# One decoder layer on one core: the output projection for prompt tile 0 first, for the rest behind two heads' queries

## The chip, the cores and the metric

One Trainium2 chip, of which the kernel uses one core. The metric is device time in microseconds, from the first to the last instruction and what lies around them, as the median of several executions. Engines are called as the profile calls them: PE (TensorE), DVE (VectorE), ACT (ScalarE), POOL (GpSimd), SP (SyncE, here only a queue of transfers).

## The reference, cut to what matters

A prompt of 256 tokens and 8 samples of one token each go through a layer of width 2048, all in f32. Three branches (a gated convolution, differential attention, attention to a memory) are gated and merged; the output projection adds them to x. Then comes PEER: queries and key scores select, for each token and each of 8 heads, 16 of 16384 experts; each expert is a row of `peer_u` and a row of `peer_v`, 8 KB each.

```python
x = x + merged @ w_o
h = rms_norm(x, norm2_w)
q = (h @ w_peer_q).reshape(n, 8, 2, 128)          # 2 x 128 per head
s1, s2 = q[:, :, 0] . sub_keys[0], q[:, :, 1] . sub_keys[1]
idx, top_s = 16 best sums of the 16 best of s1 and of s2, for each head
a = peer_u[idx] . h                                # a gathered row per token and pick
out = sum over heads and picks of softmax(top_s) * gelu(a) * peer_v[idx]
x = x + out
```

## The kernel before, in words

The 264 tokens stand as tile 0 and tile 1 of the prompt (128 each) and a tile of 8 samples. The program of each engine is written by hand; engines wait for each other on counting semaphores. The change lies behind the branches, where these parts follow each other:

- **Output projection** (PE L997 to L1003, with `chunk` L689 and `turner` L744). `w_o` comes in 8 blocks of 256 columns (2 MB) through `wring`, a ring of two slots; SP fetches block n when the second chunk of block n-2 is done (L361 to L369). A chunk is 128 output columns: 16 matmuls of 264 tokens, transposed, into a bank of `ps`. ACT copies it to `zst` (L1318), DVE adds it to the kept columns of x in `hT` (L1904) and ACT scales `hT` with the norm weight (L1321): these are the queries' operand. PE turns `zst` back to rows (three transposes), which DVE adds to `x_rows` and squares for the second norm (L1915 to L1921).
- **Queries and scores** (PE L1016 to L1038, ACT `stage_part` and `keep_scores` L1327 to L1350). `w_peer_q` has 8 blocks too, one for each head, two chunks j each (j = 2h and 2h+1). `PQ_PARTS` (L237) is their order: head 0 for tile 0, head 0 for the rest, then all heads for all tokens. Blocks 0 and 3 are loaded early into `bregion` and `oreg`, 4 and 7 into `late_h2`, the others through the ring. Each chunk is copied to `zst` by ACT, multiplied with the keys (L1013), and the scores are copied to `scores`. ACT does this in program order, and only then goes on to `winners(0)`, an exponential (L1362), and `activations(0)`, a Gelu (L1355).
- **Searches** (DVE, `search_halves`, `form_sums`, `search_sums`, `name_next`, L1966 to L2016) find the 16 experts of a head for a tile, and run between the dots, in four steps. Heads of tile 0 are g = 0 to 7, of tile 1 g = 8 to 15.
- **Gathers** (POOL L556 to L612). For each g and pick j an indirect DMA brings 128 rows of `peer_u` (1 MB) into one of four slots (`u_slots`), if the slot's earlier dot is done (`u_used`). Rows of `peer_v` go to eight slots (`e_slots`), which are parts of the weight ring, `oreg` and `hT`, so the first of them wait for query blocks (L578). Rows of v run behind those of u: `v_before` (L276), with `V_LEAD` 34. Both are issued by one program, in one order. The samples have 8 gathers of each kind of their own.
- **Dots and additions**. DVE forms the dot of each gathered u tile with `h2_rows` (L2049); `weigh(g)` (L2033) makes a head's weights from the exponential and the Gelu. The first, `weigh(0)`, stands behind the first dot of g = 2 (L2078). ACT makes a diagonal matrix of each pick's weights (L1385), PE multiplies the v rows with it and adds up in `ps` (L1057).

The second norm of tile 1 and the samples is finished at g = 5 (`late_norms`, L1933), from norm weights that SP loads over query block 7 (L386).

## Time and profile before

| | |
|---|---|
| median of 3 runs | 2703.18 us (2702.1 to 2703.5) |
| the profiled execution | 2701.93 us, span 2700.2 us |
| busy | PE 2428.8 us (90%), DVE 1474.5 (55%), ACT 349.4 (13%), POOL 806.9 (30%) |
| granted TensorE clock, mean | 0.973 |
| moved by DMA | 919.23 MB, 340 GB/s; the gather queue (q0) 725.64 MB |
| chain that ended last | PE 52%, DMA 36%, DVE 8% |

How it is read: the busy share of an engine is a mean over stages with different limits, and PE's share in particular is modelled: in the stage of the gathers its matmuls are stretched over waits. A window's row has, for one stretch of time, the busy time of each engine with its number of instructions, the granted TensorE clock (1.00 is 2.4 GHz, 0.50 is 1.2 GHz), the share of the 16 DMA engines and the rate. A row of the timeline has start, duration, engine, line, operation, written and read tile, count, and in brackets the idle time ahead of it and what ended it. A matmul in f32 stands as two records. DMA queue q0 carries the gathers, q1 the transfers that SP issues.

### The profile page before, as it was taken

The numbers are of one execution on the slowest core, as the hardware profiler recorded it, in microseconds if no ns is written. First come the engines' busy times: TensorE is split into PE (matmuls) and PEld (weight loads), VectorE is DVE, ScalarE is ACT, GpSimd is POOL, SyncE is SP. The second block draws the span as 40 slices with busy tenths as digits, with TensorE's granted clock in tenths as the row PEclk, the third lists the DMA queues.
The fourth block names the chain that finished last, engine by engine and source line by source line (L and its number), as shares of the span: only waits on it lengthen the run. The fifth ranks groups of instructions, "written<-read, shape, count | busy, mean of one in ns | idle before, by whom it ended". The sixth has DMA issues, their size and how long they took to land.

```text
span 2700.2 us, 27156 instructions
## 1 busy us (share of the span) xinstructions
PE 2428.8 (90%) x8845; PEld 1510.1 (56%) x8845; DVE 1474.5 (55%) x2290; ACT 349.4 (13%) x773; POOL 806.9 (30%) x889
## 2 busy tenths in 40 slices
PE   9999999999999999999997777777999597777778
PEld 7888886478666688888884322333433142223333
DVE  3599996842322231012487778874555555554543
ACT  2111000022222200001112110111101011111100
POOL 1122220101222200000146444544434454344442
PEclk9999999999999999999999999998989799999989
DMA  6699995865899945456599999999999999999998
GB/s 229 219 400 385 384 383 199 310 218 179 312 357 361 362 152 190 140 183 212 195 392 371 421 421 422 421 421 421 421 421 421 391 422 422 421 421 421 421 421 350
DMA packets 269444, 919.23 MB, mean 340 GB/s; under 512 B 16155, under 2 KB 122739, under 8 KB 200309
## 3 DMA queue, kind: packets, MB, share of 16 engines
q0 software_dynamic: 122448, 725.64, 66.2%
q1 hardware_dynamic: 133156, 164.93, 18.2%
q10 hardware_dynamic: 13728, 27.26, 2.7%
q8 instruction: 59, 0.97, 0.1%
q14 instruction: 53, 0.43, 0.0%
HBM read 909.08 MB, written 8.72 MB: 340 GB/s over the span
## 4 chain that ended last, share of the span: by engine, by line
PE 52%; DMA 36%; DVE 8%; issue 3%; POOL 1%; ACT 0%; DVEq 0%; POOLq 0%; ACTq 0%; SPq 0%
DMA sb_bregion<-in_peer_u_dram,sb_ring 27%; PE ps L699 13%; PE ps L807 13%; PE ps L819 6%; DVE sb_bregion L2049 4%; PE ps L689 4%; PE ps L794 4%; PE ps L1057 4%; DMA sb_mkv<-in_peer_u_dram,sb_ring 2%; PE ps L908 2%; DMA sb_S<-in_peer_u_dram,sb_ring 2%; DMA sb_wring<-in_w_in_dram 2%; DMA sb_bregion<-in_peer_v_dram,sb_ring 1%; PE ps L1031 1%; DVE sb_mkv L2049 1%
## 5 line engine op out<-in xcount | busy, mean ns | idle before, releaser
L1057 PE MATMUL ps<-sb_wring,sb_ring 128*128 128x512 f32 x992 | 456.0, 609 | 84.5 <-DMA sb_wring<-in_peer_v_dram,sb_ring 84.4
L2049 DVE CUSTOM_DVE_ANT_0 sb_bregion<-sb_bregion,sb_rows 128x2048 f32<-128x2048 f32 x128 | 293.4, 2292 | 218.5 <-DMA sb_bregion<-in_peer_u_dram,sb_ring 215.2
L699 PE MATMUL ps<-sb_hT,sb_wring 128*128 128x264 f32 x1792 | 408.2, 388 | 0.9 <-DMA sb_wring<-in_w_in_dram 0.8
L1057 PEld LDWEIGHTS ps<-sb_wring,sb_ring 128*128 128x128 f32 x992 | 185.5, 193 | 353.3 <-issue 255.3
L699 PEld LDWEIGHTS ps<-sb_hT,sb_wring 128*128 128x128 f32 x1792 | 338.6, 191 | 60.2 <-DMA sb_wring<-in_w_in_dram 2.4
L807 PE MATMUL ps<-sb_hT,sb_wring 128*128 128x264 f32 x1536 | 365.6, 389 | 1.1 <-DVEq L1418 1.1
L807 PEld LDWEIGHTS ps<-sb_hT,sb_wring 128*128 128x128 f32 x1536 | 286.4, 190 | 64.1 <-issue 16.4
L1057 PE MATMUL ps<-sb_oreg,sb_ring 128*128 128x512 f32 x496 | 236.0, 626 | 71.1 <-DMA sb_oreg<-in_peer_v_dram,sb_ring 42.8
L1057 PE MATMUL ps<-sb_hT,sb_ring 128*128 128x512 f32 x496 | 229.7, 610 | 52.0 <-DMA sb_hT<-in_peer_v_dram,sb_ring 46.7
L558 POOL DMA_INDIRECT sb_bregion<-in_peer_u_dram,sb_ring x132 | 152.1, 1152 | 328.4 <-DVEq L1418 289.7
L1385 ACT ACTIVATE sb_ring<-sb_ident,sb_ring 128x128 f32<-128x128 f32 x248 | 99.6, 401 | 912.9 <-PE ps L1057 746.5
L1057 PEld LDWEIGHTS ps<-sb_oreg,sb_ring 128*128 128x128 f32 x496 | 96.3, 200 | 209.9 <-issue 137.3
L2049 DVE CUSTOM_DVE_ANT_0 sb_S<-sb_S,sb_rows 128x2048 f32<-128x2048 f32 x64 | 146.7, 2292 | 109.7 <-DMA sb_S<-in_peer_u_dram,sb_ring 108.9
L2049 DVE CUSTOM_DVE_ANT_0 sb_mkv<-sb_mkv,sb_rows 128x2048 f32<-128x2048 f32 x64 | 147.1, 2298 | 104.3 <-DMA sb_mkv<-in_peer_u_dram,sb_ring 102.5
L1057 PEld LDWEIGHTS ps<-sb_hT,sb_ring 128*128 128x128 f32 x496 | 92.6, 193 | 187.4 <-issue 154.3
L558 POOL DMA_INDIRECT sb_wring<-in_peer_v_dram,sb_ring x128 | 156.8, 1225 | 51.5 <-issue 40.0
L1546 DVE TENSOR_REDUCE sb_S<-sb_oreg 128x1024 f32 x128 | 149.5, 1208 | 0.0
L819 PE MATMUL ps<-sb_oreg,sb_bregion 128*128 128x264 f32 x512 | 122.1, 388 | 0.0
L689 PE MATMUL ps<-sb_conv,sb_wring 128*128 128x264 f32 x512 | 116.4, 386 | 0.0
L558 POOL DMA_INDIRECT sb_S<-in_peer_u_dram,sb_ring x66 | 73.2, 1109 | 126.5 <-DVEq L1418 104.9
L819 PEld LDWEIGHTS ps<-sb_oreg,sb_bregion 128*128 128x128 f32 x512 | 96.4, 190 | 25.4 <-issue 9.4
L592 POOL COPY sb_ring<-sb_ring 128x16 int32<-128x16 int32 x16 | 18.2, 1140 | 308.5 <-DVEq L1418 308.4
(368 smaller groups left out, 2519.2 us busy)
## 6 DMA issues: line engine op xcount, KB each, us to landing
sb_wring<-in_w_in_dram SPq DMA_DIRECT2D x26, 2048.0 KB, 11.8
sb_ring<-in_cache_k_dram POOLq DMA_DIRECT2D x64, 512.0 KB, 8.5
sb_mkv<-in_cache_k_dram POOLq DMA_DIRECT2D x64, 512.0 KB, 8.5
sb_wring<-in_w_in_dram SPq DMA_DIRECT2D x26, 1024.0 KB, 12.8
sb_wring<-in_w_in_dram ACTq DMA_DIRECT2D x26, 1024.0 KB, 14.0
sb_mkv<-in_cache_v_dram POOLq DMA_DIRECT2D x48, 512.0 KB, 7.1
sb_rows<-in_cache_v_dram POOLq DMA_DIRECT2D x47, 512.0 KB, 7.6
sb_wring<-in_w_mem_kv_dram SPq DMA_DIRECT2D x8, 2048.0 KB, 8.6
```

Source lines behind the costliest of these rows:

```text
L558: nc.gpsimd.indirect_dma_start(dst, None, table, bass.IndirectOffsetOnAxis(ap=idx, axis=0)).then_inc(landed, 16)
L689: last = mm(ps[:, (2 * r + c) % 4, 0:NT], wring[:, r, k, c * P:(c + 1) * P], rhs[:, k, :], start=(k == 0), stop=(k == KC - 1))
L699: last = mm(ps[:, c, 0:NT], whalf[:, h, k % BC, c * P:(c + 1) * P], rhs[:, k, :], start=(k == 0), stop=(k == KC - 1))
L794: last = mm(ps[:, 2 * g + t, :], memT[:, k, t * P:(t + 1) * P], whalf[:, h, k % BC, :], start=(k == 0), stop=(k == KC - 1))
L807: last = mm(ps[:, c, 0:NT], wring[:, r, k, c * P:(c + 1) * P], hT[:, k, :], start=(k == 0), stop=(k == KC - 1))
L819: last = mm(ps[:, bank, 0:NT], bwring[:, r, k, c * P:(c + 1) * P], operand[:, k, :], start=(k == 0), stop=(k == BC - 1))
L908: last = mm(ps[g * QUAD:g * QUAD + w.shape[1], 6 + q, :], w, v_slots[page_slot(p)][:, q * 512:(q + 1) * 512], start=first, stop=final)
L1031: last = mm(ps[:, i % 4, lo:hi], pq_block(b, k)[:, c * P:(c + 1) * P], hT[:, k, lo:hi], start=(k == 0), stop=(k == KC - 1))
L1057: last = mm(ps[:, 4 * t + q, :], diag[:, k % 4, :], e_slots[v % ER][:, q * 512:(q + 1) * 512], start=False, stop=q_stop, skip_group_check= ...
L1385: st(A_(diag[:, k % 4, :], ident[:, :], ACT.Copy, scale=wexp[:, g % 4, j:j + 1]))
L1546: st.run(RED(out(p), by_head(prods[p % 2]), X, ALU.add))
L2049: st(V.tensor_tensor_reduce(out=u_slots[n % UR], in0=u_slots[n % UR], in1=h2, scale=1.0, scalar=0.0, op0=ALU.mult, op1=ALU.add, accum_out= ...
```

## The change

It runs the output projection in two passes. The first has the 128 columns of tile 0 alone, 16 chunks; tile 0's rows, squares and root follow as before. Then come 36 steps (`STEPS`): the queries of heads 0 and 1 for tile 0 (4 steps of 128 columns); the output projection for tile 1 and the samples (16 steps of 136 columns, blocks 7 down to 0); head 2's queries for all tokens; heads 0 and 1 for the rest (4 steps of 136 columns); heads 3 to 7 for all tokens. Blocks 7 and 6 of `w_o` are still in the ring; 5 to 0 are read a second time. In a projection step the residual is added by a 17th matmul with the identity, ACT writes the scaled column to `hT`, the turned rows to `x_rows`, and squares them. The means of these squares are taken at g = 4 and the norm at pick 8 of g = 5, with a root of their own.

Query block 0 is loaded early into `oreg` and block 1 into `late_h2`; 2, 3, 5, 6 come through the ring, 4 and 7 into `late_h2`. `V_LEAD` becomes 40, head 2's search for tile 0 begins at pick 9 of g = 1 instead of pick 3, the `peer_u` gathers no longer wait for the queries in `bregion`, and the order of four v slots changes.

```diff
         H_CONV, H_MEM, H_GATE = 8, 14, 18
         SPLIT, RESTS = 4, 7 + 6
         R_QKV, R_O, R_PQ = 0, 32, 48
-        PQ_PARTS = [(0, 0, P), (1, 0, P), (0, P, NT), (1, P, NT)] + [(j, 0, NT) for j in range(2, KC)]
-
-
-        def parts_through(n):
-
-            return max(i + 1 for i, (j, _, _) in enumerate(PQ_PARTS) if j // 2 == n)
+        O_AGAIN = [7, 6, 5, 4, 3, 2, 1, 0]
+        STEPS = [("pq", j, 0, P) for j in range(4)]
+        STEPS += [("o", 2 * n + c, P, NT) for n in O_AGAIN for c in range(2)]
+        STEPS += [("pq", j, 0, NT) for j in (4, 5)] + [("pq", j, P, NT) for j in range(4)]
+        STEPS += [("pq", j, 0, NT) for j in range(6, KC)]
+        LAST_O = max(i for i, step in enumerate(STEPS) if step[0] == "o")
+
+        def done_through(kind, n):
+
+            return max(i + 1 for i, (what, j, _, _) in enumerate(STEPS) if what == kind and j // 2 == n)
+
+        def scored_through(t, h):
+
+            return max(i + 1 for i, (what, j, lo, hi) in enumerate(STEPS) if what == "pq" and j == 2 * h + 1 and lo <= TILES[t][0] < hi)
 
         def pq_block(n, k):
 
-            if n in (4, 7):
+            if n in (1, 4, 7):
                 return pq_late[:, k // BC, k % BC, :]
-            home = {0: pq_early, 1: wring[:, 0], 2: wring[:, 1], 3: pq_oreg, 5: wring[:, 0], 6: wring[:, 1]}[n]
+            home = {0: pq_oreg, 2: wring[:, 1], 3: wring[:, 0], 5: wring[:, 1], 6: wring[:, 0]}[n]
             return home[:, k, :]
 
         PICKS = 2 * PH * TOPK
         OWN_ROUTED, OWN_HEAD = 5, 7
+        SUMMED = 4
         U_SLOTS, V_SLOTS = PICKS + TS, PICKS + TS - PH
-        V_LEAD, V_LEFT = 34, 12
+        V_LEAD, V_LEFT = 40, 12
 
         def dots_after(g, j):
...
                     sp.dma_start(hflat, xT_dram).then_inc(s["xT_back"], 16)
                 fetch(n % NR, w_o, n * BLK)
                 if n == 2:
-                    sp.dma_start(pq_early, w_pq[:, :, 0:BLK]).then_inc(pq_landed[0], 16)
-                if n == 3:
-                    sp.dma_start(pq_oreg, w_pq[:, :, 3 * BLK:4 * BLK]).then_inc(pq_landed[3], 16)
+                    sp.dma_start(pq_oreg, w_pq[:, :, 0:BLK]).then_inc(pq_landed, 16)
                 if n == 4:
                     sp.wait_ge(s["qk_stored"], 64)
-                    late_query_weights(4)
-            for n in (1, 2):
-                sp.wait_ge(s["chunk_full"], C_O + 12 + 2 * n)
-                fetch(n - 1, w_pq, n * BLK)
-            for n in (5, 6):
-                sp.wait_ge(s["chunk_full"], C_PQ + parts_through(n - 4))
-                fetch(n - 5, w_pq, n * BLK)
-            sp.wait_ge(s["chunk_full"], C_PQ + parts_through(4))
+                    late_query_weights(1)
+            for n in (5, 4, 3, 2, 1, 0):
+                sp.wait_ge(s["chunk_full"], C_PQ + done_through("o", n + 2))
+                fetch(n % NR, w_o, n * BLK)
+            for n in (2, 3):
+                sp.wait_ge(s["chunk_full"], C_PQ + done_through("o", 3 - n))
+                fetch((n + 1) % NR, w_pq, n * BLK)
+            sp.wait_ge(s["chunk_full"], C_PQ + done_through("pq", 2))
+            fetch(1, w_pq, 5 * BLK)
+            sp.wait_ge(s["chunk_full"], C_PQ + done_through("pq", 1))
+            late_query_weights(4)
+            sp.wait_ge(s["chunk_full"], C_PQ + done_through("pq", 3))
+            fetch(0, w_pq, 6 * BLK)
+            sp.wait_ge(s["chunk_full"], C_PQ + done_through("pq", 4))
             late_query_weights(7)
-            sp.wait_ge(s["chunk_full"], C_PQ + parts_through(7))
+            sp.wait_ge(s["chunk_full"], C_PQ + done_through("pq", 7))
             sp.dma_start(h2_rows[:, 1, :], A["norm2_w"][0:1, :].to_broadcast([P, D])).then_inc(s["late_rows_in"], 16)
...
 
             def gather_u(n, idx):
                 pool.wait_ge(s["u_used"], n + 1)
-                if n == 2:
-                    pool.wait_ge(s["chunk_full"], C_PQ + parts_through(0))
                 gather(peer_u, u_slots[n % UR], idx, u_landed[n % UR])
 
...
             for j in range(KC):
                 if j % 2 == 0:
                     pe.wait_ge(w_landed[j // 2 % NR], 16 * (G_O // NR + j // 4 + 1))
-                chunk(j // 2 % NR, j % 2, C_O + j, merged)
+                pe.wait_ge(s["chunk_taken"], C_O + j + 1)
+                for k in range(KC):
+                    last = mm(ps[:, j % 4, 0:P], wring[:, j // 2 % NR, k, j % 2 * P:(j % 2 + 1) * P], merged[:, k, 0:P], start=(k == 0), stop=(k == KC - 1))
+                last.then_inc(s["chunk_full"], 1)
                 if j >= 1:
-                    o_turn((j - 1) % 4, j - 1)
+                    turn_first(j - 1)
...
                     if lo <= first < hi:
-                        last = mm(ps[0:n, 4 + i % 2, t * P:(t + 1) * P], zst[:, i % 2, first:first + n], skT[:, j % 2, :], start=True, stop=True)
+                        if what == "pq":
+                            last = mm(ps[0:n, 4 + i % 2, t * P:(t + 1) * P], zst[:, i % 2, first:first + n], skT[:, j % 2, :], start=True, stop=True)
+                        else:
+                            last = nc.tensor.transpose(ps[0:n, 4 + i % 2, t * P:(t + 1) * P], zst[:, i % 2, first:first + n], ident[:, :])
                 last.then_inc(s["tr_full"], 1)
...
+                    if i == LAST_O + 1 and k in (0, 2 * O_AGAIN[-1] + 1):
+                        pe.wait_ge(s["chunk_taken"], C_PQ + 4 + LAST_O + (k > 0))
                     last = mm(ps[:, i % 4, lo:hi], pq_block(b, k)[:, c * P:(c + 1) * P], hT[:, k, lo:hi], start=(k == 0), stop=(k == KC - 1))
...
+            def output_chunk(i, j, lo, hi):
+
+                n, c = j // 2, j % 2
+                if c == 0 and n < 6:
+                    pe.wait_ge(w_landed[n % NR], 16 * (G_PQ // NR + (5 - n) // NR + 1))
+                for k in range(KC):
+                    mm(ps[:, i % 4, lo:hi], wring[:, n % NR, k, c * P:(c + 1) * P], merged[:, k, lo:hi], start=(k == 0), stop=False)
+                mm(ps[:, i % 4, lo:hi], ident[:, :], hT[:, j, lo:hi], start=False, stop=True).then_inc(s["chunk_full"], 1)
+
+            for i, (what, j, lo, hi) in enumerate(STEPS):
+                pe.wait_ge(s["chunk_taken"], C_PQ + i + 1)
+                if what == "pq":
+                    query_chunk(i, j, lo, hi)
+                else:
+                    output_chunk(i, j, lo, hi)
                 if i == 1:
                     score(0)
                     score(1)
                 if i >= 3:
                     score(i - 1)
...
             for j in range(KC):
                 act.wait_ge(s["chunk_full"], C_O + j + 1)
                 act.wait_ge(s["rows_taken"], R_O + j + 1)
-                st(A_(zst[:, j % 2, :], ps[:, j % 4, 0:NT], ACT.Copy))
+                st(A_(zst[:, j % 2, 0:P], ps[:, j % 4, 0:P], ACT.Copy))
                 act.sem_inc(s["chunk_taken"], 1)
                 act.wait_ge(s["x1T_full"], j + 1)
-                st(A_(hT[:, j, :], hT[:, j, :], ACT.Copy, scale=cols[:, 56 + j:57 + j]))
+                st(A_(hT[:, j, 0:P], hT[:, j, 0:P], ACT.Copy, scale=cols[:, 56 + j:57 + j]))
...
-            root(7, stat[:, 0:3])
-            act.wait_ge(s["scores_clear"], 1)
+            root(7, stat[:, 0:1])
...
+                what, j, lo, hi = STEPS[i]
                 act.wait_ge(s["chunk_full"], C_PQ + i + 1)
-                st(A_(zst[:, i % 2, lo:hi], ps[:, i % 4, lo:hi], ACT.Copy))
+                st.run(A_(zst[:, i % 2, lo:hi], ps[:, i % 4, lo:hi], ACT.Copy))
+                if what == "o":
+                    st.run(A_(hT[:, j, lo:hi], ps[:, i % 4, lo:hi], ACT.Copy, scale=cols[:, 56 + j:57 + j]))
+                st.settle()
                 act.sem_inc(s["chunk_taken"], 1)
...
+                what, j, lo, hi = STEPS[i]
                 act.wait_ge(s["tr_full"], R_PQ + i + 1)
                 for t, (first, n) in enumerate(TILES):
                     if lo <= first < hi:
-                        st.run(A_(scores[0:n, t, j * P:(j + 1) * P], ps[0:n, 4 + i % 2, t * P:(t + 1) * P], ACT.Copy))
+                        src = ps[0:n, 4 + i % 2, t * P:(t + 1) * P]
+                        if what == "pq":
+                            st.run(A_(scores[0:n, t, j * P:(j + 1) * P], src, ACT.Copy))
+                        else:
+                            st.run(A_(x_rows[0:n, t, j * P:(j + 1) * P], src, ACT.Copy))
+                            st.run(A_(small[0:n, t, :], src, ACT.Square, accum_out=block_sums[0:n, t, j:j + 1]))
                 st.settle()
                 act.sem_inc(s["rows_taken"], 1)
...
@@ -1399,6 +1447,8 @@
                 activations(g)
                 if g + 1 < 2 * PH:
                     winners(g + 1)
+                if g == SUMMED:
...
@@ -1888,12 +1938,11 @@
             dve.wait_ge(s["sk_full"], 1)
             st(CP(skT, ps[:, 6, 0:2 * P].rearrange("p (c d) -> p c d", c=2)))
...
+                part = x_rows[:, 0, m * P:(m + 1) * P]
+                st(TT(part, ps[:, 4 + m % 2, 0:P], part, ALU.add))
                 signal("rows_taken")
-                for t, (_, n) in enumerate(TILES):
-                    part = x_rows[0:n, t, at]
-                    st.run(V.tensor_tensor_reduce(out=cflat[0:n, t * P:(t + 1) * P], in0=part, in1=part, scale=1.0, scalar=0.0,
-                                                  op0=ALU.mult, op1=ALU.add, accum_out=block_sums[0:n, t, m:m + 1]))
-                st.settle()
-            st(RED(stat[:, 0:3], block_sums, X, ALU.add))
-            st(TSC(stat[:, 0:3], stat[:, 0:3], 1.0 / D, EPS, ALU.mult, ALU.add))
-            signal("sqrt_in")
-            st(V.memset(scores[:, 2, :], 0.0))
-            signal("scores_clear")
+                st(V.tensor_tensor_reduce(out=cflat[:, 0:P], in0=part, in1=part, scale=1.0, scalar=0.0,
+                                          op0=ALU.mult, op1=ALU.add, accum_out=block_sums[:, 0, m:m + 1]))
+
+            def mean_squares(first, last):
+
+                st(RED(stat[:, first:last], block_sums[:, first:last, :], X, ALU.add))
+                st(TSC(stat[:, first:last], stat[:, first:last], 1.0 / D, EPS, ALU.mult, ALU.add))
+                signal("sqrt_in")
+
+            mean_squares(0, 1)
             dve.wait_ge(s["sqrt_out"], 7)
-            st(REC(stat[:, 0:3], stat[:, 0:3]))
+            st(REC(stat[:, 0:1], stat[:, 0:1]))
             dve.wait_ge(s["n2_in"], 16)
             st(STT(h2_rows[:, 0, :], x_rows[:, 0, :], stat[:, 0:1], n2_w, ALU.mult, ALU.mult))
 
+            def late_sums():
+
+                dve.wait_ge(s["rows_taken"], R_PQ + 2 + LAST_O + 1)
+                mean_squares(1, 3)
+
             def late_norms():
 
-                dve.wait_ge(s["late_rows_in"], 96)
+                dve.wait_ge(s["sqrt_out"], 8)
+                st(REC(stat[:, 1:3], stat[:, 1:3]))
+                dve.wait_ge(s["late_rows_in"], 128)
                 for t, (_, n) in list(enumerate(TILES))[1:]:
                     st.run(STT(h2_rows[0:n, t, :], x_rows[0:n, t, :], stat[0:n, t:t + 1], h2_rows[0:n, t, :], ALU.mult, ALU.mult))
                 st.settle()
...
 
             def search_halves(t, h):
 
-                if t == 0:
-                    dve.wait_ge(s["rows_taken"], R_PQ + 2 + 2 * h + (4 if h else 2))
-                else:
-                    dve.wait_ge(s["rows_taken"], R_PQ + 2 + len(PQ_PARTS))
+                dve.wait_ge(s["rows_taken"], R_PQ + 2 + (scored_through(0, h) if t == 0 else len(STEPS)))
                 find_eight(list(halves_of(t, h)))
...
                         own_dot(dots_after(g, j - 1))
                     if j == 0 and g == 2:
                         weigh(0)
-                    if j == 0 and g == 5:
+                    if j == 0 and g == SUMMED:
+                        late_sums()
...
                     if g + 1 < 2 * PH:
-                        t, h, first = (g + 1) // PH, (g + 1) % PH, 3 if g else 4
+                        t, h, first = (g + 1) // PH, (g + 1) % PH, {0: 4, 1: 9}.get(g, 3)
```

## Rows read from the trace of the kernel before

**Rows 1.** Windows: PE, PEld, DVE, ACT, POOL busy, PEclk, DMA share, GB/s

```profile
1329.80:1450.70 120.90, 114.32 (x531) 92.72 (x529) 92.93 (x137) 21.82 (x68) 67.59 (x40) 1.00 0.95 365
1450.70:2690.00 1239.30, 992.27 (x2124) 396.61 (x2125) 749.57 (x1255) 141.82 (x304) 559.10 (x503) 0.95 1.01 419
...
2140.00:2160.00 20.00, 16.75 (x34) 7.42 (x35) 11.38 (x10) 3.01 (x6) 5.77 (x5) 0.81 0.80 317
```

**Rows 2.** Gather queue, 1328 to 1450.7, then 1450.7 to 2700.2: packets, MB, share

```profile
q0 software_dynamic: 5011, 36.60, 75.8%
...
q0 software_dynamic: 71021, 517.09, 99.5%
```

**Rows 3.** ACT: the group of its score copies; its first Gelu in the timeline

```profile
L1340 ACT ACTIVATE sb_conv<-ps 128x128 f32<-128x128 f32 (+1 forms) x48 | 9.5, 267 | 103.5 <-PE ps L1013 103.3
...
1445.36 0.22 ACT L1355 ACTIVATE sb_ring<-sb_ring 128x16 f32<-128x16 f32 x1
```

**Rows 4.** Timeline of POOL and DVE: first gather, dots 1 and 26, weigh(0)

```profile
1329.80 1.02 POOL L558 DMA_INDIRECT sb_mkv<-in_peer_u_dram,sb_ring  x1 [0.96 <-POOL sb_ring L592]
...
1335.31 2.29 DVE L2049 CUSTOM_DVE_ANT_0 sb_mkv<-sb_mkv,sb_rows 128x2048 f32<-128x2048 f32 x1 [6.44 <-DMA sb_mkv<-in_peer_u_dram,sb_ring]
...
1424.91 2.29 DVE L2049 CUSTOM_DVE_ANT_0 sb_S<-sb_S,sb_rows 128x2048 f32<-128x2048 f32 x1 [0.19 <-DVE sb_ring L2049]
...
1450.68 0.17 DVE L2038 TENSOR_REDUCE sb_ring<-sb_ring 128x1 f32<-128x16 f32 x1
```

**Rows 5.** Timeline of PE: projection, parts of 128 and 136 columns, whole chunks

```profile
1213.20 7.29 PE L689 MATMUL ps<-sb_conv,sb_wring 128*128 128x264 f32 x32
1220.33 0.49 PE L744 MATMUL ps<-sb_ident,sb_zst 128*128 128x128 f32 x3
1220.65 7.29 PE L689 MATMUL ps<-sb_conv,sb_wring 128*128 128x264 f32 x32
...
1310.05 1.06 PE L1031 MATMUL ps<-sb_hT,sb_bregion 128*128 128x128 f32 x8
...
1317.53 0.39 PE L1013 MATMUL ps<-sb_mkv,sb_zst 128*128 128x128 f32 x2
...
1318.43 7.58 PE L1031 MATMUL ps<-sb_hT,sb_bregion 128*128 128x136 f32 x64
...
1342.40 7.39 PE L1031 MATMUL ps<-sb_hT,sb_wring 128*128 128x264 f32 x32
...
1350.48 7.39 PE L1031 MATMUL ps<-sb_hT,sb_wring 128*128 128x264 f32 x32
...
1440.62 1.03 PE L1013 MATMUL ps<-sb_mkv,sb_zst 128*128 128x128 f32 x6 [1.23 <-ACTq L1332]
```

**Rows 6.** Fetch of w_o block 1; a window of full load; all eight w_o fetches

```profile
L309 SPq DMA_DIRECT2D sb_wring<-in_w_o_dram x1: 427/427/427, 1189.8 to 1189.8; - x1
...
DMA to landing us min/median/max: 13.9/13.9/13.9
...
1210.00:1213.00 3.00, 3.00 (x16) 2.53 (x15) 0.00 (x0) 0.00 (x0) 0.00 (x0) 1.00 1.10 351
...
sb_wring<-in_w_o_dram SPq DMA_DIRECT2D x8, 2048.0 KB, 8.1
```

**Rows 7.** Two query fetches among gathers, 1341.7 and 1357.9; queues until 1376.4

```profile
DMA to landing us min/median/max: 18.5/22.4/26.3
...
q0 software_dynamic: 1294, 9.42, 67.6%
q1 hardware_dynamic: 4128, 4.19, 36.1%
```

**Rows 8.** PE after idle time: its timeline, then two windows of 3 us

```profile
1455.80 6.60 PE L1057 MATMUL ps<-sb_oreg,sb_ring 128*128 128x512 f32 x8 [9.74 <-DMA sb_oreg<-in_peer_v_dram,sb_ring]
...
1458.00:1461.00 3.00, 3.00 (x4) 1.01 (x3) 2.68 (x4) 0.00 (x0) 2.70 (x2) 0.50 1.00 415
1461.00:1464.00 3.00, 3.00 (x8) 1.33 (x7) 1.99 (x10) 0.40 (x1) 2.17 (x3) 0.88 1.02 423
```

More of the change, by code:

```diff
@@ L293, in build @@
         AREA = ps[:, 3:6, :].rearrange("p a b -> p (a b)")
+        block_sums = small[:, 0, 0:3 * KC].rearrange("p (t m) -> p t m", t=3)
         block = ctx.enter_context(nc.Block())
@@ L996, in _, with turn_first @@
             last.then_inc(s["sk_full"], 1)
-            o_turn = turner(C_O, R_O)
+            def turn_first(j):
+                pe.wait_ge(s["chunk_taken"], C_O + 4 + j + 1)
+                pe.wait_ge(s["rows_taken"], R_O + j + 1)
+                nc.tensor.transpose(ps[:, 4 + j % 2, 0:P], zst[:, j % 2, 0:P], ident[:, :]).then_inc(s["tr_full"], 1)
             for j in range(KC):
@@ L1347, in _ @@
             keep_scores(1)
-            for i in range(2, len(PQ_PARTS)):
+            for i in range(2, len(STEPS)):
                 stage_part(i)
@@ L1401, in _ @@
                     winners(g + 1)
+                if g == SUMMED:
+                    root(8, stat[:, 1:3])
                 if g == OWN_ROUTED:
@@ L1890, in _ @@
             signal("sk_ready")
-            dve.wait_ge(s["x_again"], 32)
+            dve.wait_ge(s["x_again"], 16)
             st.run(V.memset(zero512, 0.0))
@@ L1895, in _ @@
             st.run(CP(iota_f, iota_i))
-            block_sums = small[:, 0, 0:3 * KC].rearrange("p (t m) -> p t m", t=3)
             st(V.memset(block_sums, 1.0))
@@ L1903, in add_columns @@
                 dve.wait_ge(s["chunk_taken"], C_O + 4 + j + 1)
-                st(TT(hT[:, j, :], zst[:, j % 2, :], hT[:, j, :], ALU.add))
+                st(TT(hT[:, j, 0:P], zst[:, j % 2, 0:P], hT[:, j, 0:P], ALU.add))
                 signal("x1T_full")
@@ L1911, in _ @@
                 dve.wait_ge(s["tr_full"], R_O + m + 1)
-                at = slice(m * P, (m + 1) * P)
-                src = ps[:, 4 + m % 2, 0:2 * P].rearrange("p (t n) -> p t n", t=2)
-                own = ps[0:TS, 4 + m % 2, 2 * P:3 * P]
-                st.run(TT(rows[:, 0:2, at], src, rows[:, 0:2, at], ALU.add))
-                st(TT(rows[0:TS, 2, at], own, rows[0:TS, 2, at], ALU.add))
-                signal("rows_taken")
-                for t, (_, n) in enumerate(TILES):
-                    part = x_rows[0:n, t, at]
-                    st.run(V.tensor_tensor_reduce(out=cflat[0:n, t * P:(t + 1) * P], in0=part, in1=part, scale=1.0, scalar=0.0,
-                                                  op0=ALU.mult, op1=ALU.add, accum_out=block_sums[0:n, t, m:m + 1]))
@@ L2078, in _ @@
                         weigh(0)
-                    if j == 0 and g == 5:
+                    if j == 0 and g == SUMMED:
+                        late_sums()
+                    if j == 8 and g == SUMMED + 1:
                         late_norms()
```

39 lines of the change are left out of this document (17 added, 22 removed).

## The prediction

> **What bounds the kernel now.** I read it from the end backwards. The windows by stage [rows 1] show the last 1239 us, from 1450.7 to 2690, with the 16 DMA engines at 1.01 of their time and 419 GB/s, while DVE works 750 us of it and PE's matmuls wait for rows. That stage is bound by the expert gathers; after it come 10.2 us of last additions and stores. The stage ahead of it, 1329.8 to 1450.7, runs at 365 GB/s: DVE forms indices and dots, only `peer_u` rows are gathered, PE still makes queries. Everything before 1329.8 on this path is PE's. The queue totals [rows 2] say how much is gathered when: 36.60 MB before 1450.7, 517.09 MB after, in all 528 gathers of 1.0486 MB. At the full rate of 421.5 GB/s (419 less the hole below) the 517.09 MB take 1226.8 us; so 12.5 us of the 1239.3 are holes, 4 of them in 2140 to 2160 [rows 1], where tile 0 hands over to tile 1.
>
> So the end is a sum: time X at which the gathers run freely, plus the bytes left at 421.5 GB/s, plus 12.5, plus 10.2. Before: 1450.7 + 1226.8 + 12.5 + 10.2 = 2700.2, the profiled span. The median of the runs, 2703.2, lies 3.0 above that span; I add 3.0 at the end.
>
> What is X? L2078 puts `weigh(0)` behind the first dot of head 2, the 33rd dot. It waits for ACT's first exponential and first Gelu, and ACT's program has these behind the whole loop over the query steps (L1348, then `winners(0)`, `activations(0)`). Before, ACT had them out at 1445.6 [rows 3] and DVE ended dot 33 and weighed at 1450.7 [rows 4], so that nothing waited. No `peer_v` row can be used before `weigh(0)`, and `peer_u` rows can only be four ahead of the dots. The change edits neither line. This is the hinge of what follows.
>
> **The part that comes sooner.** A chunk of the output projection (264 columns) and its turns repeat every 7.45 us: 7.12 for 32 records and 0.33 for three turns [rows 5]. A query part of 128 columns takes 7.48 us for two, so 3.74 each; 136 columns take 3.79 each (7.58 for 64 records) [rows 5]. A tile 0 chunk with one turn is then 3.85, a block (two chunks) 7.7, and 16 chunks 61.6 instead of 119. But the blocks now follow each other faster than they come. w_o block 1 lands at 1189.8 + 13.9 = 1203.7 [rows 6], with its slot freed by the work ahead, as before: PE, done with block 0 at 1198.9, waits 4.8. A block of 2.097 MB at the 350 GB/s that these fetches reach takes 6.0, from issue to landing 8.1 when alone [rows 6]. In the queue stand block 2, query block 0, block 3, block 4, query block 1 in two halves, blocks 5, 6, 7. At 6.0 each: block 2 lands 1210, query block 0 at 1216, block 3 at 1222 (PE waits 3), block 4 at 1228, query block 1 at 1234, block 5 at 1240 (waits 3), 6 at 1246, 7 at 1256 (8.1 after block 5 is used up). PE ends tile 0 at about 1264; between 1253 (no waits) and 1270 (landings 6.6 apart). Before, the first query part began at 1310.05 [rows 5], so the last chunk had ended at 1309.7: 46 sooner. From there to the first gather the steps are the same, 20.1 us [rows 4, 5]; the memset of the sample scores that goes from DVE ran beside two query parts, so nothing. First gather 1284 instead of 1329.8, first dot about 1290.
>
> **The part that comes later.** PE's work up to the last scores, without any wait for weights: steps 0 and 1 7.5, steps 2 and 3 with scores 8; 16 chunks of 136 columns, each 3.79 + 0.24 (the identity matmul, two records) + 0.22 (two turns) = 4.25, 68; then query block 2 whole, 16.2 (8.08 a chunk [rows 5]); four parts of 136 columns, 16; ten whole chunks, 80.8. That is 196.5: from 1264 to 1461. Before, the last chunk ended at 1440.6. So even unhindered PE ends 20 later, since halving the columns costs 10, the weight queue 12, and the rest nearly cancels.
>
> It will be hindered. From 1284 gathers run, and PE needs w_o blocks 5 to 0 and query block 2 through a ring of two slots: a slot is refilled while the other block's two chunks (8.5 us) run. Alone a fetch takes 8.1, just enough. Among gathers, the two that before has took 26.3 and 18.5; the two together, 4.19 MB, took from 1341.7 to 1376.4, 17.4 each, while the gathers moved 9.42 MB [rows 7]. In that stretch the DMA engines were full. So with both slots loading a cycle is 8.5 + 25 for two blocks. Blocks 7 and 6 are kept: PE works to 1297; block 5 is issued at 1288.5 and lands at 1313, 4 at 1323, 3 at 1347, 2 at 1357, 1 and 0 at about 1374 to 1380, sooner than the cycle says, because DVE stops: its next search (head 2, after 26 dots) needs query block 2. 26 dots took until 1427.2 from 1335.3 with two searches [rows 4], about 80 with one, so it stops near 1370 to 1385, and the gathers with it. Query block 2 lands near 1392, is done at G = 1408. Bounds for G: 1364 (the fetches never slowed, the 196.5 above) and 1425 (30 gathers at 2.49 and 7 blocks at 6.0 are 117 us of DMA from 1286, landings in the worst order, then two chunks). I take 1408, near the rows of [rows 7]. From G: 16 + 80.8 = 97, and 0 to 9 for query block 4, fetched only behind the four parts. PE ends at 1505 (1461 to 1531). ACT's last copies, two table loads, exponential and Gelu add 5 [rows 3]: `weigh(0)` at X = 1510.
>
> DVE reaches dot 33 about 30 us after G, at 1440, and waits 70. By then 37 gathers (33 + 4 ahead) are moved, 38.8 MB: 2.2 MB more than before at its X. So 514.9 MB are left, 1221.6 us. Restarting costs: the four slots are empty, the first new row lands 5 us after `weigh(0)`, and `peer_v` starts only at gather 40: 8 us (0 to 12).
>
> **Sum**: 1510 + 8 + 1221.6 + 12.5 + 10.2 = 2762.3, and 3.0 for the median: 2765.
>
> **Cover and small edits.** The nine added blocks among the gathers (12 are fetched behind 1284, three before) cost 54 us of DMA time at 6.0, all in the time when DVE waits anyway; without that wait they would be on the path. ACT has six operations in a projection step where a query step had up to four. A copy takes 0.27 and ACT sat idle 103 us before 48 of them [rows 3]; six, with the two sums of the squares and its own waits, are some 2.6 us by that row, against 4.25 a step: hidden, with about 1.5 to spare in the chain turn, copy, stage, turn. The second root, later `late_norms` and the fourth wait count on `late_rows_in` lie in DMA-bound time where DVE is idle 40% [rows 1]: nothing. The last norm rows (SP, behind the queries) load during DVE's wait. Lead 40 instead of 34 puts `peer_v` six gathers later; at the tile switch that may fill the 4 us hole of 2140 (0 to 4 gained, I take 0); the last gathers have the same order.
>
> The Trainium skill bears on the contention (DMA: Bandwidth & Descriptors, Queues, rings and completion order): an engine goes round-robin between its queues, a packet at a time. The rows agree that neither queue is served first: weights had 36.1% and gathers 67.6% of the engines. Were weights served first instead, the sum would be 2722.
>
> **Rivals.** (a) Weights are not slowed: G at 1364, X at 1466, 2718 + 3 = 2722. For it: DVE leaves gaps while it searches. Against: 18.5 and 26.3 [rows 7]. (b) The clock falls as well. After PE's 9.7 us of idleness the granted clock went to 0.50, 1.2 GHz, until some 6 us after work began again [rows 8]; PE now idles 6 to 10 us before most of seven blocks. At 6 us of half clock each loses 3; a longer hold doubles whole blocks, 8.5 each: 10 to 40 later, 2775 to 2805, centre 2790. The skill names this pattern (TensorE: Matmul & The Clock Gate, HAM oscillation: a wait for DMA before each tile lets it start at the low clock). (c) Faster: the gathers are what bounds from their first one on, and DVE isn't held at dot 33. Then start 46 sooner, 54 of weights more, and the hole of 1329.8 to 1450.7 filled (365 against 421.5 GB/s, 16 us): 2703 - 46 + 54 - 16 = 2695; with the weights in DVE's gaps down to 2657. It decides where ACT's first Gelu is out before dot 33; for that PE would have to end before about 1400, against 1461 at the very best. (d) It doesn't do what it says: the first gather isn't earlier, since the weight queue holds tile 0's projection. Up to 30 us of delay there are absorbed by DVE's wait as far as DVE goes, but push PE too: 2775 to 2795.
>
> **Chances.** Forecast 0.62 (own range 2745 to 2785), (a) 0.14, (b) 0.13, (c) 0.05, (d) 0.04, no visible change by sums that cancel 0.02. The range 2722 to 2796 takes in (a) and most of (b). The measurement tells 0.2% (5 us): slower 0.93, same 0.03, faster 0.04.
>
> **What would show it.** First gather near 1284; PE's projection chunks with 7.1 us replaced by 3.7, with idle before blocks 1, 3, 5; landings of the reread blocks at 15 to 26 us and PE idle on `in_w_o_dram`; DVE idle for tens of us twice, before a search and before L2038, released by ACT; 37 gathers moved by then; full rate after it. I am wrong if DVE isn't idle before L2038, or if PE's last scores come before 1455.

## The result, and the profile after

The changed kernel takes 2794.34 us (median; 2790.28 to 2794.86) against 2703.34 for the kernel before, timed beside it: ratio 1.0331, 95% interval 1.0316 to 1.0347. It is 91 us slower; the forecast was 62 slower, 2765, with a range up to 2796. The direction held; the size was 29 short.

The windows of the kernel after, with the columns of [rows 1], over the stretch in question:

```profile
1189.00:1264.00 75.00, 60.74 (x500) 59.21 (x499) 13.70 (x60) 9.50 (x28) 0.00 (x0) 0.93 0.87 281
1264.00:1290.00 26.00, 25.81 (x229) 25.62 (x228) 13.73 (x50) 5.62 (x16) 2.44 (x4) 1.00 0.04 9
1290.00:1400.00 110.00, 53.95 (x391) 52.51 (x390) 68.34 (x87) 16.22 (x88) 53.01 (x29) 0.74 1.03 394
1400.00:1450.00 50.00, 48.84 (x337) 44.77 (x337) 9.95 (x29) 10.46 (x53) 1.88 (x2) 0.96 0.49 158
1450.00:1500.00 50.00, 50.00 (x243) 41.60 (x242) 14.68 (x21) 5.41 (x22) 10.48 (x6) 1.00 0.73 253
1500.00:1550.00 50.00, 37.37 (x169) 28.89 (x168) 10.56 (x20) 14.82 (x37) 5.55 (x3) 0.93 0.14 53
```

Until 1400 the DMA engines are full and PE works half of the time. Then it turns round: PE is full up to its last scores, DVE works 35 of 150 us, and the rate falls to 158, 253 and 53 GB/s, where before, from 1450.7 on, it was 419 [rows 1]. The transfers began sooner and then stood idle.

Where the two halves meet is in the timelines of DVE and POOL (start, duration, engine, line, operation, tiles, idle time ahead and what ended it):

```profile
1287.13 1.03 POOL L571 DMA_INDIRECT sb_mkv<-in_peer_u_dram,sb_ring  x1 [0.95 <-POOL sb_ring L603]
...
1439.47 0.49 DVE L2003 MAX8 sb_mkv<-sb_conv 128x8 f32<-128x128 f32 x2 [57.38 <-ACTq L1390]
...
1537.29 0.17 DVE L2088 TENSOR_REDUCE sb_ring<-sb_ring 128x1 f32<-128x16 f32 x1 [71.03 <-ACTq L1411]
...
1542.59 2.43 POOL L571 DMA_INDIRECT sb_S<-in_peer_u_dram,sb_ring  x1 [74.27 <-DVEq L1468]
```

The first gather comes 43 us sooner than in [rows 4]. DVE waits 57 us at its search for head 2 and 71 at `weigh(0)` (L2088 here, L2038 before), and POOL with it. The second wait ends when ACT, done with its score copies, gives out its first exponential and Gelu: the order that [rows 3] showed with nothing waiting on it.

The queue totals of the kernel after, from 1287 to 1538.7, and from there to the end:

```profile
q0 software_dynamic: 5328, 38.80, 38.9%
...
q0 software_dynamic: 70704, 514.88, 98.9%
```

### The profile page after: what moved, and what is told of

Same layout as the page of the kernel before. It is cut to its first block, busy times and chain, and to the rows that moved or that the text cites. A ratio compares the mean times of both kernels' runs of the same rounds, so it can differ in the third digit from the quotient of the medians.

```text
span 2792.1 us, 28495 instructions
## 1 busy us (share of the span) xinstructions
PE 2450.3 (88%) x9453; PEld 1549.9 (56%) x9453; DVE 1459.2 (52%) x2212; ACT 371.5 (13%) x905; POOL 814.7 (29%) x888
## 4 chain that ended last, share of the span: by engine, by line
PE 53%; DMA 34%; DVE 8%; issue 3%; POOL 2%; ACT 0%; DVEq 0%; POOLq 0%; SPq 0%; ACTq 0%
DMA sb_bregion<-in_peer_u_dram,sb_ring 16%; PE ps L710 13%; PE ps L818 12%; PE ps L830 6%; DMA sb_S<-in_peer_u_dram,sb_ring 5%; DMA sb_wring<-in_w_o_dram 5%; PE ps L1056 4%; PE ps L1098 4%; DMA sb_mkv<-in_peer_u_dram,sb_ring 4%; PE ps L805 3%; DVE sb_bregion L2099 3%; PE ps L919 2%; PE ps L1065 2%; DMA sb_bregion<-in_peer_v_dram,sb_ring 1%; DMA sb_wring<-in_peer_v_dram,sb_ring 1%
## 5 line engine op out<-in xcount | busy, mean ns | idle before, releaser
L1065 PE MATMUL ps<-sb_conv,sb_wring 128*128 128x136 f32 x512 | 72.0, 306 | 56.0 <-DMA sb_wring<-in_w_o_dram 56.0
L571 POOL DMA_INDIRECT sb_mkv<-in_peer_u_dram,sb_ring x66 | 75.8, 1149 | 132.2 <-DVEq L1468 118.9
L805 PE MATMUL ps<-sb_wring,sb_bregion 128*128 128x512 f32 x256 | 110.3, 592 | 1.3 <-DMA sb_wring<-in_w_mem_kv_dram 1.3
```

The costliest lines, as they stand in the source:

```text
L571: nc.gpsimd.indirect_dma_start(dst, None, table, bass.IndirectOffsetOnAxis(ap=idx, axis=0)).then_inc(landed, 16)
L805: last = mm(ps[:, 2 * g + t, :], memT[:, k, t * P:(t + 1) * P], whalf[:, h, k % BC, :], start=(k == 0), stop=(k == KC - 1))
L1065: mm(ps[:, i % 4, lo:hi], wring[:, n % NR, k, c * P:(c + 1) * P], merged[:, k, lo:hi], start=(k == 0), stop=False)
```

## Experiments

Each time stands beside the kernel before, run on the same chip in the same job (2703.5 to 2706.8 us); the ratio is to that. A point of time is from a kernel's one profiled execution, a measured time is the median of four runs unless more are named. "X" is the start of `weigh(0)`. Theory A is the prediction's: time lost is PE's delay, handed to X. Rival B is that the gathers' own path (bytes, restarts) sets it.

**1. Without the second reads.** SP's six fetches and PE's waits on them are left out (the counts that the later waits on the ring expect are lowered to match, not shown), so part of the result is left out too:

```diff
-                fetch(n % NR, w_o, n * BLK)
...
-                if c == 0 and n < 6:
-                    pe.wait_ge(w_landed[n % NR], 16 * (G_PQ // NR + (5 - n) // NR + 1))
```

> Edit: the changed kernel without the six fetches that read w_o blocks 5 to 0 again, and without PE's waits for them; the projection of tile 1 and the samples is computed from whatever lies in the ring, so that part of the result is left out. Theory A (the end follows the time X at which DVE gets past weigh(0), and X is PE's end plus about 6 us): the 56 us of waits on w_o and some 10 us of half clock go, head 2's queries are done near 1367 instead of 1433, X falls from 1539 to about 1473, and the time to about 2728, still 25 above the kernel before. Rival B (the added traffic is what costs, as DMA time): 12.6 MB at 350 GB/s are 36 us, so 2758. Rival C (something behind X, such as V_LEAD 40, costs): the full-rate stage would be longer than 1253 us from X.

Measured 2744.24, ratio 1.0147 (1.0126 to 1.0167): 50 us faster than after, X at 1488.5. The time lies between theory A's 2728 and rival B's 2758, so by itself it decides nothing; X does. The gain is that of X (from 1537.3 to 1488.5, 48.8), DVE still stood 71.2 us at `weigh(0)`, as in the kernel after, so that DMA time saved ahead of it could gain nothing there, and from X to the end it was 1255.9 us for the 1254.8 of the kernel after (rival C is out). But X came 15 later than expected. PE's timeline in this kernel shows why: query block 2 was now the fetch that stood among the gathers. It was issued at 1341.4 and took 26.0 to land, and PE went on at 1367.5 (the trace names no releaser for it; the times meet).

```profile
1367.53 2.98 PE L1055 MATMUL ps<-sb_hT,sb_wring 128*128 128x264 f32 x6 [17.64 <-issue]
```

**2. Gathers held back.** POOL waits for the end of tile 1's projection before its first gather; nothing is left out:

```diff
             v = 0
+            pool.wait_ge(s["chunk_full"], C_PQ + done_through("o", 0))
             for g in range(2 * PH):
```

> Edit: the changed kernel with one wait more on POOL: the first gather is issued only when the projection of tile 1 and the samples is done, some 65 us later than in the changed kernel. Nothing is left out. Theory A: the rereads land in 8 to 9 us each, PE has nearly no waits in that part and ends near 1467 instead of 1532; the gathers lose 65 us of a time that DVE spent waiting anyway, DVE reaches dot 33 about 115 us after its first dot, near 1475, and the time is 2725 to 2740, 55 to 70 faster than the changed kernel although its gathers start 65 later. Rival B (the gathers are the bound from their first one on): 65 us later, 2794 to 2860.

Measured 2737.12, ratio 1.0117 (1.01 to 1.0134). The first gather was 67 us later than in the kernel after, and the end 57 us sooner. The six reads landed as these lines of their group say, issues 1291.9 to 1335.8, with query block 2 among them:

```profile
  PE ps L1066: 2.0, 3
...
DMA to landing us min/median/max: 8.1/8.2/9.3
```

PE waited 2.0 us for them in all, its last scores began at 1470.2, and nothing waited at `weigh(0)`, which came at 1480.7. The time is in theory A's range, 57 below where rival B's begins. In this kernel the early start lost more through PE than it gave. But the gathers now begin at 1354.0, 24 later than in the kernel before, and PE's last scores, hardly hindered, still 29.6 later (1440.62 there): with the gathers held, nothing of the change's gain is left.

**3. The price of PE's delay alone.** Before, with 45 idle matmuls ahead of the first chunk of query block 7:

```diff
             for i, (j, lo, hi) in enumerate(PQ_PARTS):
                 b, c = j // 2, j % 2
+                if j == 14:
+                    warm(45)
```

> Edit: the kernel before with 45 idle matmuls of 512 columns (0.88 us each, about 40 us) on PE ahead of the first chunk of query block 7. No transfer is added. Theory A: ACT's first Gelu comes out near 1485 instead of 1445.6, DVE waits some 35 us before weigh(0), 38.8 MB are moved by then, and the time is 2703 + 34 to 38 = 2737 to 2741. Rival B (bandwidth alone decides): the gathers run on meanwhile and at most the few us until the slots are full are lost, 2703 to 2718.

Measured 2733.8, ratio 1.0106 (1.0089 to 1.0123): 28 to 30 slower where 34 to 38 was expected, X at 1483.9 after a wait of 30.09 us for the exponential.

```profile
1483.90 0.17 DVE L2040 TENSOR_REDUCE sb_ring<-sb_ring 128x1 f32<-128x16 f32 x1 [30.09 <-ACTq L1365]
```

PE's last scores began 39.9 later (1480.48 for 1440.62) and X came 33.2 later: the kernel before has a reserve of 6.7 us on PE, no more. Its profiled span grew by 31.3 (2731.5 for 2700.2), since the stretch from X to the end took 1247.6 instead of 1249.5; the median moved by 28. The forecast of 34 to 38 had taken this reserve as 2 to 6. Most of the 3 us between 31.3 and 28 is that the kernel before took 2705.71 in this job and 2703.18 in the one of its profile.

**4. ACT's first Gelus inside its step loop**, in the kernel after (and out of their old place behind it):

```diff
...
             for i in range(2, len(STEPS)):
                 stage_part(i)
                 keep_scores(i)
+                if i == LAST_O + 2:
+                    winners(0)
+                    activations(0)
+                    winners(1)
+                if i == LAST_O + 10:
+                    activations(1)
+                    winners(2)
...
```

> Edit: the changed kernel with ACT's first exponentials and Gelus taken into its loop over the steps: winners 0 and 1 and activations 0 behind the scores of head 2, winners 2 and activations 1 eight steps later. Theory A: DVE no longer stops behind dot 33 but behind dot 41, at the first search for the samples, which needs the last scores. POOL then has 45 rows of u and 3 to 6 of v issued instead of 37 of u, 11 to 14 gathers of 2.49 us: 27 to 35 us earlier, less up to 5 us of table loads between PE's steps, so 2760 to 2772. Rival: it is the slots of the v rows and not weigh(0) that holds the gathers; then no more than the 8 rows of u, 20 us, or nothing, 2774 to 2794.

Measured 2758.45, ratio 1.0194 (1.0177 to 1.0211), 36 faster than after and just below the expected range: `weigh(0)` ran at 1468.6. The wait moved on, as expected, to DVE's next searches (95.8 us in three of them) and to `peer_v` rows, 19.9 us of POOL waiting for PE's blocks. The order on ACT is a second, smaller cause; PE's delay stays. The distance from PE's last scores to the end says how much each is worth. Where `weigh(0)` waits for ACT (the kernel after and experiments 1, 6 and 9) it is 1258.0 to 1259.4 us; in the four kernels with this edit (4, 7, 8 and 10) 1221.6 to 1222.0. So PE's end sets the time in all eight, and ACT's order adds 36 to it.

**5. V_LEAD 40 in the kernel before** (`V_LEAD, V_LEFT = 40, 12`).

> Edit: the kernel before with V_LEAD 40 instead of 34 and nothing else. Theory A: the v rows come six gathers later, so that fewer of them wait for slots when tile 0 hands over to tile 1 (the window 2140 to 2160, at 317 instead of 421 GB/s): 0 to 4 us faster, 2699 to 2704 where the kernel before has 2703. Rival: the later v rows lengthen the end or leave DMA without work early on, 5 us or more slower; then a part of the loss of the change is V_LEAD's.

Measured 2707.85 (11 runs) against 2704.89 (15 runs), ratio 1.001 (1.0001 to 1.0019). Not the gain allowed for; 3 us lost at most.

**6. PE kept at work through the waits**, in the kernel after:

```diff
+                if c == 0 and n in (5, 3, 2, 1):
+                    warm({5: 22, 3: 18, 2: 9, 1: 3}[n])
                 if c == 0 and n < 6:
```

> Edit: the changed kernel with idle matmuls of 512 columns on PE ahead of four waits for reread blocks: 22 before block 5, 18 before 3, 9 before 2, 3 before 1, each a little shorter than the wait that the changed kernel shows there (22.0, 19.0, 9.8, 4.6 us). Theory: the first chunk behind each wait runs at the full clock, 3.9 us instead of 6.8, 5.8, 5.9 and 6.9, since PE wasn't idle; as each block's end releases the next fetch, most of the 10 us is on the path: X falls from 1539 to about 1530 and the time from 2794 to 2784 to 2788. Rival: the fetches alone set the pace, and the time stays within 2 us of 2794.

Measured 2796.47, ratio 1.0332: no gain. The idle matmuls were too few to fill the waits, and in what was left of them the granted clock still fell to 0.50. PE's timeline in this kernel (idle matmuls L635, then the first chunk of block 5), and the window of that chunk's first 3 us:

```profile
1300.50 19.05 PE L635 MATMUL ps<-sb_ones,sb_ident 128*128 128x512 f32 x44
1325.44 5.62 PE L1067 MATMUL ps<-sb_conv,sb_wring 128*128 128x136 f32 x32 [5.89 <-DMA sb_wring<-in_w_o_dram]
...
1325.50:1328.50 3.00, 3.00 (x13) 3.00 (x14) 2.81 (x3) 0.00 (x0) 0.17 (x1) 0.50 1.12 389
```

The chunk ended at 1331.1; in the kernel after, without idle matmuls, at 1329.4. Whether waits filled to the end would give back the 2 to 3 us for each chunk stays open, and so does why the fetches landed a little later here, after 33.1 us (median of seven).

**7 and 8. The first gather after block 2, or after block 4,** of tile 1's projection, with edit 4. The wait of experiment 2 becomes

```diff
+            pool.wait_ge(s["chunk_full"], C_PQ + done_through("o", 2))
```

(and the same with 4 for 2)

> Edit: the changed kernel with the early exponentials of e4_early_act and the first gather held back until the projection of block 2 is done (near 1335), between the 1287 of the changed kernel and the 1354 of e2_gathers_wait. Theory A: two rereads and query block 2 still meet gathers, some 10 us of PE waits, PE ends near 1480; DVE is held neither at dot 33 nor, much, at dot 41; by 1481 some 42 gathers are moved: 1481 + 486 times 2.49 + 23 + 3 = 2717, range 2708 to 2730, so faster than either edit alone (2737, 2758) and slower than the kernel before. Rival: once weigh(0) no longer holds DVE, an earlier start pays fully, and e9_o4_early is faster than this one by its 17 us.

> Edit: as e8_o2_early, with the first gather held back until the projection of block 4 is done (near 1318). Theory A: four rereads meet gathers, PE ends 15 to 25 us later than in e8_o2_early, DVE waits at dot 41 for the last scores, and the time is the same or up to 15 us longer, 2715 to 2740. Rival (an earlier start pays fully): 2690 to 2705.

Measured 2746.06, ratio 1.015 (1.0132 to 1.0168), and 2742.99, ratio 1.0136 (1.012 to 1.0151). The first missed its expectation (2708 to 2730) by 16, the second (2715 to 2740) by 3, and the second isn't faster by the rival's 17, nor slower. PE's last scores came at 1520.78 and 1523.17, not near 1480 and 1500. In the first kernel PE waited 9.85 us for `w_o` block 0 and 13.5 for query block 2, where 10 had been expected for all, and 14.1 for query block 4, which I had not counted; in the second 22.9 for query block 2 (issued at 1369.4, landed after 31.4) besides 23.6 for `w_o`. PE's timeline, query block 4 in the first kernel and query block 2 in the second:

```profile
1453.12 3.30 PE L1057 MATMUL ps<-sb_hT,sb_rows 128*128 128x264 f32 x7 [14.12 <-DMA sb_rows<-in_w_peer_q_dram]
```

```profile
1400.88 3.42 PE L1057 MATMUL ps<-sb_hT,sb_wring 128*128 128x264 f32 x7 [22.94 <-issue]
```

**9. Two gathers in flight.** By now every loss led back to one number, the landing time of a 2 MB block among gathers. This asks what sets it: in the kernel after, a gather of the first 26 waits for the dot two before it instead of four.

```diff
-                pool.wait_ge(s["u_used"], n + 1)
+                pool.wait_ge(s["u_used"], n + (3 if 2 <= n < 26 else 1))
```

> The kernel after, with only two peer_u gathers in flight instead of four for the first 26 (a gather waits for the dot two before it, not four before it); nothing is left out. What it asks: why do the second reads of w_o land 25 to 39 us after their issue, the term that the forecast missed. Theory A, they stand behind the gathers that are already queued: with half as many, landings of 14 to 22 us, PE's waits in the projection 25 to 35 us instead of 56, PE's last scores near 1510, weigh(0) near 1515 instead of 1539, end 24 earlier: about 2770 (2760 to 2780). The slower gathers cost nothing, since DVE still waits for head 2's queries. Rival B, the weight queue gets its share whatever the number of gathers, as long as one is there: landings stay at 25 to 39, end 2788 to 2800.

Measured 2753.15, ratio 1.0173 (1.0156 to 1.019): 41 us faster than after, 7 below theory A's range (24 had been expected), and rival B is out. PE's last scores began 41.8 sooner (1492.09 for 1533.86). The six reads in this kernel:

```profile
  PE ps L1065: 20.2, 3
...
DMA to landing us min/median/max: 13.0/14.9/16.1
```

The queues from 1292 to 1342, first the kernel after, then this one (packets, MB, share of the 16 engines):

```profile
q0 software_dynamic: 2006, 14.62, 72.9%
q1 hardware_dynamic: 4867, 4.95, 29.6%
```

```profile
q1 hardware_dynamic: 8256, 8.39, 52.0%
q0 software_dynamic: 1232, 8.91, 44.3%
```

The engines were full in both (1.03 and 0.97 of their time); only the split changed, and with it PE's work. DVE's dots waited 87 us for rows and lost nothing by it: it was no longer held at head 2's search, and 28.14 us instead of 71.03 at `weigh(0)`, X at 1495.5. From the end of that wait, 1497.2, to the end it was 1253.2 us, as in the kernel after (1253.1).

**10. Gathers held back and ACT's edit together** (2 and 4).

> The first gather held until the projection of tile 1 is done, and besides ACT's first exponentials and Gelus inside its step loop (both edits of the runs before, together); nothing is left out. With the gathers held alone, weigh(0) was not waited for (2737), so the theory that the two waits are one and the same cost, PE's end, expects no more than noise: 2733 to 2741. The rival, that ACT's place in the program has a price of its own behind the gathers, expects 2720 to 2730.

Measured 2754.82 (2742.59 to 2765.78), ratio 1.0192 (1.0158 to 1.0227): outside both expectations, some 18 slower than 2 alone by the medians. My edit had laid a trap of its own. ACT's timeline in this kernel: the first Gelu waits for DVE's first 16 dots, which were late since the gathers were, and every score copy stood behind it.

```profile
1414.87 0.22 ACT L1400 ACTIVATE sb_ring<-sb_ring 128x16 f32<-128x16 f32 x1 [38.16 <-DVEq L1476]
```

```profile
1417.29 1.32 PE L1035 MATMUL ps<-sb_mkv,sb_zst 128*128 128x128 f32 x4 [40.38 <-ACTq L1376]
```

PE then stood still for 40 us, later for 6.5 more at query block 4, and its last scores began at 1519.16 instead of 1470.2. The profiled execution is the fastest of the four; what the others lost beyond it, up to 23 us, no trace shows. In 7 and 8, which have edit 4 too, PE waited 3.5 us for ACT in all; what held it there was weights.

**11. Two in flight, and ACT's first Gelu alone, six steps behind the projection** (9, and edit 4 cut to `winners(0)`, `activations(0)`, `winners(1)` at `LAST_O + 6`, late enough for the dots).

> Two gathers in flight, as in the run before, and ACT's first exponential and first Gelu (head 0 alone) inside its step loop, six steps behind the projection of tile 1; nothing is left out. There DVE waited 28.1 us for ACT ahead of weigh(0), the same wait that holds the gathers in the kernel after. Theory A, that wait is what is left of the cost: weigh(0) at 1467 instead of 1495.5, no other wait of the size, end = 1467 + 2 + 1253 + 2 = 2724 (2718 to 2732). Rival B, the wait is handed on, to v rows that wait for PE's query blocks (before the last chunk at 1482) or to PE, whose fetches then run among v rows as well: end 2735 to 2750. Theory C, the bytes that the change adds ahead of the free stretch (26.3 MB of weights and 38.8 of rows from 1287) allow a time below the kernel before: under 2700.

Measured 2730.53, ratio 1.0095 (1.0061 to 1.0129): in theory A's range. Nothing waits at `weigh(0)` any more, which ran at 1471.2 (DVE's timeline in this kernel):

```profile
1470.98 0.08 DVE L2103 DVE_READ_ACCUMULATOR2_ANT sb_ring<- 128x1 f32 x1
1471.21 0.17 DVE L2092 TENSOR_REDUCE sb_ring<-sb_ring 128x1 f32<-128x16 f32 x1
```

With this, 64 of the 91 us are undone with all of the change in place. No version beat the kernel before. An estimate from the other versions says what was left: they end no sooner than 1254 after X (experiment 2) and 1222 after PE's last scores (4, 7, 8 and 10). Here that is 1471.2 + 1254 = 2725 and 1496.9 + 1222 = 2719, with 2730 measured. To come below the 2700 of the kernel before, both the 33rd dot and PE's end would have to be sooner.

## Why the prediction was right in direction and 29 us short

By its own steps:

- **Tile 0's projection, 1264**: 1268.1. The waits came before blocks 1, 3, 5 and 7 as said, 5.47, 1.28, 5.16 and 0.86 us. What the sum left out is that the first chunk after the two longer waits ran slower, 5.55 and 5.27 instead of 3.74 us. Everything upstream was 1.3 later. First gather 1287.13 for 1284: right.
- **The second projection, G = 1408**: 1433.2. **This is the step that failed.** I took 1408, near the two landings of 18.5 and 26.3 in [rows 7]. PE's chunks in the kernel after, and the windows of the beginning and the end of the first one:

```profile
1322.53 6.82 PE L1065 MATMUL ps<-sb_conv,sb_wring 128*128 128x136 f32 x32 [21.97 <-DMA sb_wring<-in_w_o_dram]
...
1329.64 3.87 PE L1065 MATMUL ps<-sb_conv,sb_wring 128*128 128x136 f32 x32
...
1362.18 5.80 PE L1065 MATMUL ps<-sb_conv,sb_wring 128*128 128x136 f32 x32 [18.99 <-DMA sb_wring<-in_w_o_dram]
...
1322.50:1325.50 3.00, 2.97 (x13) 3.00 (x14) 2.53 (x7) 0.00 (x0) 1.35 (x1) 0.50 0.99 386
1328.50:1331.00 2.50, 2.50 (x24) 2.48 (x23) 2.31 (x3) 1.04 (x7) 2.43 (x1) 1.00 1.01 393
```

  The first five reads took 30.3, 34.1, 28.3, 39.2 and 25.0 us, and PE waited 56.0 for them, where the forecast has 44 of waits (1408 less the 1364 without any). Blocks 5, 4, 3 and 2 landed at 1322, 1335, 1362 and 1382 for the 1313, 1323, 1347 and 1357 of the forecast, and query block 2 at 1417 for 1392. [rows 7] was the right place to look but the wrong size to take from it: there the weights had 36.1% of the engines and moved 4.19 MB in 34.7 us, here 29.6% and 4.95 MB in 50 us (the queues from 1292 to 1342 in experiment 9), less for each us by a fifth. The other term that was missing is the slow chunks: four, of 6.82, 5.80, 5.94 and 6.86 us for 3.87, 9.9 in all, each with a granted clock of 0.50 in its first microseconds.

  The upper bound for G, 1425, was passed as well. It laid all the bytes end to end at full rate. But query block 2 needs a slot of the ring, and was issued only when `w_o` block 1 had been used:

```profile
L319 SPq DMA_DIRECT2D sb_wring<-in_w_peer_q_dram x1: 367/367/367, 1408.8 to 1408.8; - x1
...
DMA to landing us min/median/max: 8.3/8.3/8.3
```

  By then the gathers had stopped and the engines had run out of work: the window from 1400 to 1450 has them at 0.49.
- **From G to PE's end, 97 us, and 5 to X**: 98.5 to the end of the last chunk at 1531.7, with no wait at query block 4, and 7.3 to 1539.0, where `weigh(0)` has its Gelu. 3.8 over.
- **The hinge, `weigh(0)` behind ACT's loop**: right in mechanism and place. Predicted 1510; it began at 1537.3, and its second wait, for the Gelu, ended at 1539.0. The first wait is 71.03 us (predicted 70; dot 33 and X both came later than predicted, so that the 29 don't show in it), and DVE stopped before a search after dot 26 as well (57.38 us).
- **Bytes before X, 38.8 MB, and 514.9 after**: 38.80 and 514.88. **Restart, holes and tail, 1252.3 from X**: 1253.1 from 1539.0. Right.
- **Cover and small edits**: ACT kept up with the projection steps: no chunk of PE there waited for it. The reads cost on the path only what they delayed PE; experiment 1 gave 50 for them, all of it in X.
- **V_LEAD, 0 to 4 gained**: 0 to 3 lost in the kernel before (experiment 5).

So the miss of 29 (1539.0 for 1510) is 1.3 upstream, 2.8 in tile 0's part, 21.1 from there to G (25.2 in G, less those 4.1) and 3.8 behind it. Of the rivals, (a), weights not slowed, is refuted by the five landings of 25.0 to 39.2 us; its mechanism came about only when the gathers were held (experiment 2). (b), the clock, gave a number near the result (2790), partly for the wrong reason, and a part of it came true beside the forecast's own mechanism. The granted clock did fall (0.74 from 1290 to 1400), and the slow chunks are 9.9 of the 21.1 us and 3.3 more in tile 0's part: 13 of the 29, if each is on the path, which is argued from the order of the fetches and not shown by a run; the rest is later landings. Experiment 6 doesn't settle what a steady clock would have given. (c), faster, is out: DVE was held at dot 33. (d) is out: the first gather came sooner.

The Trainium skill (TensorE: Matmul & The Clock Gate, HAM oscillation) says that waits for DMA between tiles let the clock drop each time. This trace agrees for its longer waits: 6.82, 5.80, 5.94 and 6.86 us for a chunk of 3.87, after waits of 21.97, 18.99, 9.78 and 4.64.

Experiments 2, 9 and 11 say what the change ran into: PE, with two ring slots, had only 6.7 us of reserve in this stretch already before (experiment 3), the change gives it more to do (its last scores 29.6 later even when the gathers were held), and gathers whose dots were not needed yet took the DMA engines from the weights that PE waited for.

## What to carry to other kernels

Before you start a transfer stream earlier, ask what will be the last to be ready for its results, and whether the stream takes from that one. Here the gathers started 43 us sooner and the kernel lost 91, and half as many in flight gave 41 back. A fetch among other transfers has no fixed price: the same block took 13.0 to 16.1 us beside two gathers and 25.0 to 39.2 beside up to four; and a landing read from another stretch is a guess until both queues' shares are compared. When an edit moves a wait forward in an engine's program, look at what stands behind it (experiment 10: 40 us of PE).

## What the runs showed of the hardware that was not expected

- A 2 MB block of weights landed in 8.1 to 9.3 us alone, 13.0 to 16.1 among two gathers in flight, 25.0 to 39.2 among up to four (18.3 at most among two in experiment 11; down to 18.2 among four in experiment 7, up to 48.5 in 6). Here the share that a queue got depended on how much the other had in flight: weights went from 29.6% to 52.0% of engines that were full or nearly so when the gathers' number was halved. I had treated it as a fixed split.
- After a wait of 4.64 us PE's granted clock was 0.50 (1397.6 to 1401.0) and the chunk took 6.86 instead of 3.87 us; after one of 1.28 us it was 1.00 (1223.3 to 1227.1) and the chunk took 3.84 for 3.74. The chunk behind 18.99 us of waiting was shorter, 5.80, than the one behind 4.64: what a wait costs didn't grow with its length.
